# Gated results turned by VectorE and GpSimd instead of TensorE, with the first two output chunks taken in turns

## The reference

```
h = rmsnorm(x)                      # layers 2, 3: also scaled and shifted
q, k, v, ..., z = split(h @ w_in)   # 2048 -> 6400 .. 20480 columns
mixed = mixer(q, k, v, ...)         # (256, 2048)
gated = mixed * silu(z)
x = x + gated @ w_out               # layers 2, 3: times a gate row
```

## Time and profile before

| | |
|---|---|
| time, median of 3 runs (lowest, highest) | 2493.15 us (2492.67, 2493.81) |
| time of the profiled execution | 2495.73 us |
| its span, first to last instruction | 2493.9 us |
| busy: PE, DVE, ACT, POOL | 2452.6, 1703.0, 1184.6, 522.9 us |
| mean granted TensorE clock | 0.995 |
| HBM traffic over the span | 212 GB/s |

### The profile page before, as it was taken

The page is one execution under the profiler, slowest core; times in us unless marked ns, Lnnn a source line. Parts: engine busy times, 40 slices in busy tenths (PEclk is TensorE's granted clock), DMA queues, the critical chain, the costliest instruction groups (busy, mean ns, idle before and its releaser), DMA issues.

```text
span 2493.9 us, 30840 instructions
## 1 busy us (share of the span) xinstructions
PE 2452.6 (98%) x11830; PEld 2055.0 (82%) x11830; DVE 1703.0 (68%) x2086; ACT 1184.6 (48%) x1573; POOL 522.9 (21%) x692
## 2 busy tenths in 40 slices
PE   8999999999999999999999999999999989999998
PEld 7898888888888887888888888888888878888786
DVE  5887865677787776666566666666655676667665
ACT  5557654445445544344443434444454444444543
POOL 1000000134430000533153053234300023223000
PEclk9999999999999999999999999999999999999999
DMA  7545545687767875887588677768745657777654
GB/s 237 167 136 148 149 129 188 188 269 252 250 219 242 269 260 169 271 268 253 168 257 259 202 248 242 236 210 262 252 137 181 193 176 229 226 228 228 203 193 136
DMA packets 254468, 531.80 MB, mean 213 GB/s; under 512 B 16377, under 2 KB 26945, under 8 KB 254193
## 3 DMA queue, kind: packets, MB, share of 16 engines
q1 hardware_dynamic: 253120, 526.06, 66.9%
q0 software_dynamic: 896, 3.20, 0.4%
q10 hardware_dynamic: 304, 0.57, 0.1%
HBM read 527.67 MB, written 2.10 MB: 212 GB/s over the span
## 4 chain that ended last, share of the span: by engine, by line
PE 81%; issue 11%; DVE 4%; ACT 2%; POOL 1%; DMA 0%; POOLq 0%; DVEq 0%; SPq 0%; ACTq 0%
PE proj L1020 23%; PE proj L1022 23%; PE proj L1021 23%; PE att L1070 2%; PE att L1053 2%; DVE w_lo L1697 1%; PE proj L1001 1%; ACT w_hi L1298 1%; PE att L1201 1%; PE att L1117 1%; PE proj L1006 1%; POOL slot L2001 1%; PE proj L1027 1%; PE proj L1028 1%; PE proj L1029 1%
## 5 line engine op out<-in xcount | busy, mean ns | idle before, releaser
L1697 DVE TENSOR_TENSOR w_lo<-raw,w_hi 128x1024 fp32r<-128x1024 f32 x804 | 989.8, 1235 | 579.6 <-ACT w_hi L1298 575.9
L1020 PE MATMUL proj<-w_hi,h 128*128 128x512 f32 (+1 forms) x3080 | 1227.8, 399 | 5.9 <-DVE h L1844 4.5
L1298 ACT ACTIVATE w_hi<-raw 128x1024 fp32r<-128x1024 f32 x804 | 847.6, 1057 | 767.2 <-PE proj L1022 747.4
L1022 PE MATMUL proj<-w_hi,h 128*128 128x512 f32 (+1 forms) x3080 | 1199.9, 390 | 0.0
L1021 PE MATMUL proj<-w_lo,h 128*128 128x512 f32 (+1 forms) x3080 | 1197.8, 389 | 0.0
L1020 PEld LDWEIGHTS proj<-w_hi,h 128*128 128x128 f32 x3080 | 580.2, 188 | 122.2 <-issue 9.7
L1022 PEld LDWEIGHTS proj<-w_hi,h 128*128 128x128 f32 x3080 | 579.3, 188 | 123.0
L1021 PEld LDWEIGHTS proj<-w_lo,h 128*128 128x128 f32 x3080 | 580.6, 189 | 114.0 <-issue 1.7
L2001 POOL COPY slot<-stage 32x256 f32<-32x256 f32 x640 | 481.1, 752 | 816.5 <-DVE stage L1714 781.1
L1858 DVE SCALAR_TENSOR_TENSOR mod_acc<-raw,vec,mod_acc 128x1024 f32<-128x1024 f32 x192 | 255.2, 1329 | 0.3 <-DMA raw<-in_mod_w 0.3
L1987 POOL TENSOR_TENSOR row_rstd<-row_rstd,power 128x2 f32<-128x2 f32 x5 | 3.6, 716 | 569.0 <-DVE row_rstd L1788 569.0
(11 more groups left out here) (236 smaller groups left out, 1486.2 us busy)
## 6 DMA issues: line engine op xcount, KB each, us to landing
raw<-in_a_w_in SPq DMA_DIRECT2D x320, 512.0 KB, 4.7
raw<-in_mod_w SPq DMA_DIRECT2D x192, 512.0 KB, 4.4
raw<-in_w_in_odd SPq DMA_DIRECT2D x128, 512.0 KB, 4.6
raw<-in_b_w_in SPq DMA_DIRECT2D x128, 512.0 KB, 4.3
raw<-in_w_in_even SPq DMA_DIRECT2D x100, 512.0 KB, 3.7
raw<-in_w_out_even SPq DMA_DIRECT2D x32, 512.0 KB, 4.1
raw<-in_w_out_odd SPq DMA_DIRECT2D x32, 512.0 KB, 5.4
raw<-in_a_w_out SPq DMA_DIRECT2D x32, 512.0 KB, 4.0
```

What stands on the lines that cost most here:

```text
L1020: pe.matmul(o, x_hi[:, xs], hi[:, kk, :], start=start, stop=False)
L1022: done = pe.matmul(o, x_lo[:, xs], hi[:, kk, :], start=False, stop=stop)
L1298: act.activation(m.w_hi[u.n % SPLIT_N][:, 0:size], m.raw[i][:, 0:size], ACT.Copy).then_inc(s.hi_ready, 1)
L1697: dve.tensor_tensor(m.w_lo[ring][:, 0:size], m.raw[i][:, 0:size], m.w_hi[ring][:, 0:size].bitcast(F32), ALU.subtract).then_inc(s.lo_dve, 1)
```

## The change

PE's hout is gone. At each of the 16 gates DVE, after its multiplication, transposes the chunk into `stage` with two instructions (one for each tile of 128 tokens), and POOL moves it with 16 copies back into `mixed`, in place. hout keeps its ACT and DVE halves, which now read `mixed` in place of the PSUM bank and wait for `turned`; they stand five slots behind the gate, not two. The turns of gates and of q and k chunks are numbered together, and each DVE transposition waits for the turn before it. The first two output chunks are run in turns: pairs 1 to 4 of the order for chunk 0, the same for chunk 1, then pairs 5 to 8 for chunk 0 and for chunk 1. With it the residual addition of chunk 0 (`resid`) moves four slots back in every layer, and so do `masks` (layer 1) and the first `weigh` (layer 3).

```diff
+    def run_in_turns(self, chunks, early, late):
+        for pairs in (early, late):
+            for c in chunks:
+                for pair in pairs:
+                    self.units.append(Unit(len(self.units), c, pair, pair * UNIT_K, pair == early[0], pair == late[-1]))
+                c.last = len(self.units) - 1
...
+    early, late = list(order)[:PAIRS // 2], list(order)[PAIRS // 2:]
+    plan.run_in_turns(cs[:2], early, late)
+    for ch in cs[2:]:
         plan.run(ch, order)
...
-        slot = max(ready[p][0] + 2, free, before + 1)
+        slot = max(ready[p][0] + TURN_SLOTS, free, before + 1)
...
         elif kind == "hin":
             use(it, kind, it.banks, s.h_done, it.n + 1)
-        elif kind == "hout":
-            use(it, kind, it.banks, s.h_done, it.n + 1)
...
-        elif kind == "hout":
-            w.wait_ge(s.gated, it.ready)
-            for j in range(UNIT_K):
-                k = it.pair * UNIT_K + j
-                for tile in range(TILES):
-                    at = j * SEQ + tile * P
-                    done = pe.transpose(m.bank(it.banks[0], at, at + P), m.mixed[:, tile, k * P:(k + 1) * P], m.ident)
-            done.then_inc(s.h_mm, 1)
...
         elif kind == "hout":
-            w.wait_ge(s.h_mm, it.n + 1)
+            w.wait_ge(s.turned, it.chunk.turn_out)
             w.wait_ge(s.unit_done, it.h_free)
             hi = m.halves(it.n % H_RING)[0]
-            act.activation(m.in_order(hi, it.layer), m.in_tiles(m.bank(it.banks[0])), ACT.Copy).then_inc(s.h_hi, 1)
+            act.activation(m.in_order(hi, it.layer), m.mixed_pair(it.pair), ACT.Copy).then_inc(s.h_hi, 1)
...
             dve.tensor_tensor(out, out, m.token(c.slot), ALU.mult).then_inc(s.gated, 1)
+            w.wait_ge(s.gated, c.gate_n)
+            w.wait_ge(s.turned, c.turn_out - 1)
+            for tile in range(TILES):
+                blocks = m.stage[:, :].rearrange("p (g t h j) -> p t g h j", g=QUAD, t=TILES, j=FOLD)[:, tile, :, :, :]
+                done = dve.transpose(blocks, out[:, tile, :].rearrange("p (h g j) -> p g h j", g=QUAD, j=FOLD))
+            done.then_inc(s.stage_full, 1)
...
-        elif kind == "turn":
+        elif kind == "turn" or kind == "gate":
             c = it.chunk
-            w.wait_ge(s.stage_full, c.turn_n)
+            n, into = (c.turn_n, m.turn_into) if kind == "turn" else (c.turn_out, m.turn_out_into)
+            w.wait_ge(s.stage_full, n)
```

More of the change, by code:

```diff
@@ L38 @@
 AHEAD = 3
+TURN_SLOTS = 5
 HEAD_PAIRS = 2
@@ L184 @@
     turn_n: int = 0
+    turn_out: int = 0
     scaled: bool = False
@@ L228 @@
     dve_n: int = 0
+    mm_n: int = 0
     act_n: int = 0
@@ L306, in out_projection @@
     for c in range(D // CHUNK):
-        ch = plan.chunk(layer, 2 * layer + 1, w, c * CHUNK, "token", "resid", col=c * CHUNK)
+        cs.append(plan.chunk(layer, 2 * layer + 1, w, c * CHUNK, "token", "resid", col=c * CHUNK))
+    early, late = list(order)[:PAIRS // 2], list(order)[PAIRS // 2:]
+    plan.run_in_turns(cs[:2], early, late)
+    for ch in cs[2:]:
         plan.run(ch, order)
-        cs.append(ch)
     return cs
@@ L404, in halves @@
         for j in range(2):
-            ready[ch.col // 256 + j] = (gated[i], ch.gate_n)
+            ready[ch.col // 256 + j] = (gated[i], ch)
     before = 0
@@ L409, in halves @@
         free = h["last"][m - H_RING] + 1 if m >= H_RING else 0
-        slot = max(ready[p][0] + 2, free, before + 1)
+        slot = max(ready[p][0] + TURN_SLOTS, free, before + 1)
         before = slot
         assert slot < min(u.n for u in plan.units if u.chunk.phase == 2 * layer + 1 and u.pair == p), (layer, p, slot)
-        plan.at(slot, "hout", layer=layer, pair=p, n=m, banks=(2 + m % 2,), h_free=free,
-                ready=ready[p][1])
+        plan.at(slot, "hout", layer=layer, pair=p, n=m, h_free=free, chunk=ready[p][1])
         h["index"][2 * layer + 1, p] = m
@@ L572, in make_plan @@
     for c in range(D // CHUNK - 1):
-        plan.at(ends[-1] - PAIRS * (2 - c) - 4, "weigh", n=c)
+        plan.at(outs[c].last + 4, "weigh", n=c)
     plan.at(ends[-1], "final")
@@ L587, in number @@
 def number(plan, s, h):
+    turns = 0
+    for slot in sorted(plan.slots):
+        for kind, it in sorted(plan.slots[slot], key=lambda w: ORDER.index(w[0])):
+            if kind == "turn":
+                turns += 1
+                it.chunk.turn_n = turns
+            elif kind == "gate":
+                turns += 1
+                it.chunk.turn_out = turns
     out_n = {"slot": 0, "resid": 0, "feature": 0}
@@ L597, in number @@
                 c.wide_n = out_n["wide"] = out_n.get("wide", 0) + 1
-        if c.form == "turn":
-            out_n["turn"] = c.turn_n = out_n.get("turn", 0) + 1
         if c.turn_n and c.layer >= 2:
@@ L640, in number @@
         elif kind == "hin":
+            it.mm_n = n
             if it.layer >= 2:
                 it.ready = count["val"] = count.get("val", 0) + 1
-            use(it, kind, it.banks, s.h_done, it.n + 1)
-        elif kind == "hout":
             use(it, kind, it.banks, s.h_done, it.n + 1)
@@ L757, in halves, with mixed_pair, staged @@
         return self.h[:, place, :, 0, :], self.h[:, place, :, 1, :]
-    def in_tiles(self, a):
-        return a.rearrange("p (k a n) -> p k a n", k=UNIT_K, a=TILES)
+    def mixed_pair(self, pair):
+        return self.mixed[:, :, pair * UNIT_K * P:(pair + 1) * UNIT_K * P].rearrange("p a (k n) -> p k a n", k=UNIT_K)
+    def staged(self, a, g):
+        return self.stage[a * FOLD:(a + 1) * FOLD, g * TURN:(g + 1) * TURN].rearrange("p (t h j) -> p t h j", t=TILES, j=FOLD)
     def in_order(self, h, layer):
@@ L801, in turn_into, with turn_out_into @@
     def turn_into(self, c, a):
-        return self.slots[c.slot][:, :].rearrange("p (b a j) -> p b a j", a=QUAD, j=FOLD)[:, :, a, :]
+        return self.token(c.slot).rearrange("p t (h a j) -> p t h a j", h=HPC, j=FOLD)[:, :, :, a, :]
+    def turn_out_into(self, c, a):
+        return self.mixed[:, :, c.col:c.col + CHUNK].rearrange("p t (h a j) -> p t h a j", h=HPC, j=FOLD)[:, :, :, a, :]
     def keys(self):
@@ L1359, in scalar_program @@
                 if j == 1 or not it.fine:
-                    w.wait_ge(s.h_mm, it.n + 1)
+                    w.wait_ge(s.h_mm, it.mm_n)
                 ps = m.bank(it.banks[j if it.fine else 0])
@@ L1848, in vector_program @@
             hi, lo = m.halves(place)
-            dve.tensor_tensor(m.in_order(lo, it.layer), m.in_tiles(m.bank(it.banks[0])), m.in_order(hi, it.layer).bitcast(F32),
+            dve.tensor_tensor(m.in_order(lo, it.layer), m.mixed_pair(it.pair), m.in_order(hi, it.layer).bitcast(F32),
                               ALU.subtract).then_inc(s.h_done, 1)
@@ L1999, in gpsimd_program @@
                     g = (a + turn) % QUAD
-                    src = m.stage[a * FOLD:(a + 1) * FOLD, g * TURN:(g + 1) * TURN].rearrange("p (b j) -> p b j", j=FOLD)
-                    done = pool.tensor_copy(m.turn_into(c, a)[g * FOLD:(g + 1) * FOLD, :, :], src)
+                    done = pool.tensor_copy(into(c, a)[g * FOLD:(g + 1) * FOLD], m.staged(a, g))
                     if a < QUAD - 1:
@@ L2009, in gpsimd_program @@
                     w.wait_ge(s.pool_step, own.n)
-                    w.wait_ge(s.turned, c.turn_n)
+                    w.wait_ge(s.turned, n)
         elif kind == "rot_norm":
```

1 line of the change is left out of this document (removed).

## The result

| | before | after |
|---|---|---|
| time, median (lowest, highest) | 2493.48 us (2492.67, 2494.34), 4 runs | 2480.88 us (2479.68, 2481.91), 4 runs |
| profiled execution, its span | 2495.73, 2493.9 us | 2479.68, 2477.9 us |

The change makes the kernel faster by 12.6 us; the ratio is 0.9949 [0.9937, 0.9961].

A forecast was written before the change was run, and what follows sets the result against it. PE's issue time was taken to bound the output projections. Gains of 14.7, 1.4, 0.8 and 1.7 us (18.6) less 4.2 lost in layer 0 gave -14.4: 2481.3 us profiled, 2478.8 as a median, range 2475 to 2486.

The forecast's parts named there:

- Issue time, -14.7: Output projections: PE no longer issues 32 houts' transposes, 27 at 0.48 us and five at 0.35, gaining 14.7 us.
- Bank waits, -1.4 and -0.8: PE's waits for a hout's lo half at L1119 and L1090 vanish, gaining 1.4 of 1.9 us and 0.8 us.
- DVE's two transpositions, 1.36 us: At each of 16 gates DVE's two added transpositions take 1.36 us together; no loss to PE was counted.
- Case (c): Rival: DVE's 1.36 us at eight gates among attention steps each cost PE in full; 2489.7 us, no change; chance 0.08.
- Copies into `mixed`: POOL's 16 copies a gate take the same durations as its existing copies, 0.445 us each where DVE is idle.
- rival (b): Copies into `mixed` take longer, turns slower by a factor; gain gone at 1.36, 2505 us at 1.6; chance 0.08.
- Layer 0: Last two gates: the second waits for an 8.6 us turn, so PE waits 2.5 us at unit 105; 4.2 lost with clock.
- Rival (a): Layer 0's turn takes 13.45 us, PE waits 7.4 and the loss is 9.1 us; 2483.7 us; chance 0.20.
- The clock, -1.7 and +1.7: PE's low clock behind L1119's wait goes, gaining 1.7 us; one behind layer 0's new wait comes, losing 1.7.
- case (d): Layer 0's clock doesn't fall or unit 105's split slips in earlier; 2476 to 2477 us; shares chance 0.62 with main forecast.
- Layers 1 to 3, "cost: nothing": Last gate of each layer: a turn may take 16.2 us before PE waits, even 15.50 fits, so nothing is lost.
- The offset of 2.6 us between the profiled execution and the median: The profiled execution before was 2.6 us over the median; subtracting this turned 2481.3 into 2478.8 us.

The follow-up runs named there:

- no_transpose: The kernel before with nobody transposing the gated results, order and spacing unchanged, so the output projection multiplies a wrong matrix; 2472.66 us, ratio 0.9919 to before.
- Experiment 5: The changed kernel with the old order of output chunks and houts two slots behind the gate, not five; 2507.82 us, ratio 1.0062 to before.
- Experiment 3: The changed kernel with layer 0's last gate transposing into another free buffer, so it does not wait for the first turn; 2478.0 us, ratio 0.9944 to before.
- order_only: The kernel before with only the new order in turns of the first two output chunks, transposes kept on PE; 2493.15 us, ratio 1.0 to before.
- experiment 4: The changed kernel with houts six slots behind their gate, not five; 2480.29 us, ratio 0.995 to before.
- experiment 7: The changed kernel with houts six slots behind the gate and layer 0's last gate keeping its eight transposes on PE; 2475.1 us, ratio 0.9925 to before.

## Why the prediction was right, and where it was off

2478.8 us was forecast, in a range of 2475 to 2486, and 2480.88 measured; in differences, -14.4 and -12.6.

2480.88 us lies inside the range, but not every term held: two terms for the clock were wrong and cancelled, and a loss that was put at nothing was in part made up by gains that were larger than forecast. That the difference came within 2 us is to that extent luck.

**Issue time, -14.7: right.** Units start 2.72 us apart, and each hout between two weight matmuls gives back 0.48 to 0.49 us. no_transpose, with nothing put in the transposes' place, bounds all gains together: 18.9 us in the ledger, of which the issue time and the two bank waits of the sum are 16.9.

**Bank waits, -1.4 and -0.8: right.** For L1119's wait of 1.9 us a rest of 0.5 was foreseen, for DVE's copy that now stands behind the gate's transpositions. The rest is what L1144 waits for that same copy (L1681 now): 0.28 us by the printed wait, 0.5 by the ledger (a step of -2.04 us, and -2.58 in no_transpose).

**DVE's two transpositions, 1.36 us: right.** They take 1.30. Case (c) did not come: at the early gates, where the forecast took nothing, attention steps lose this 0.5 us in layer 0 and 0.4 at L1248 in layer 3 (the wait is 0.8 in no_transpose and 1.2 in every kernel that turns that gate), not 10.9.

**Copies into `mixed`: right.** The 256 of them take 180.8 us, 706 ns each, against 752 ns for those into a slot, and those that fall in DVE's idle time take 390 to 400 ns. So the factor of rival (b) is not above 1, and its mechanism is absent. The turns took 8.99 to 15.25 us, two of them above the 14 that stood among the signs. The Trainium skill's rule (VectorE: DVE Perf Modes, Rules for kernel authors) to give a 128x128 transposition to TensorE did not hold here: TensorE's issue bounds the time (98% busy), and the two engines that took it over were busy for only 70% and 28% of it. Experiment 5 shows that turns can nevertheless make this kernel slower: for want of distance, not of speed.

**Layer 0: right in mechanism, 0.7 us short in size.** A wait of 2.5 us was forecast, 3.20 measured. The turn took 8.99 us and not 8.6. And it began 8.37 us before PE came to the unit (370.54, and 382.11 - 3.20 = 378.91), not 8.65. Together 0.7. The second part comes from the gate: it starts 0.15 us behind the first weight matmul of unit 101 (367.92 and 367.77), where before it started 0.37 ahead of it (374.60 and 374.97). Of these 0.5 us, 0.2 are given back, as the printed wait takes PE to come that much later than the pitch of 2.72 has it. Why the gate came later was not tried. Rival (a) with its turn of 13.45 us did not come, for the reason that stood against it: DVE is blocked in just this stretch. Experiment 3 is the counter-test: with DVE not blocked, the turn took 12.71. (That most turns of before take 13.45 us is not so either: of the 40, 22 took less, from 8.98 to 13.39, and nine 13.45 or 13.46.)

**The clock, -1.7 and +1.7: both wrong as steady terms.** The low clock behind the 1.9-us wait was a property of that execution: a second one of the same kernel and order_only have the same wait of 1.88 us, and 1.00 behind it. Behind the wait of 3.20 us in after the clock stayed up, behind 3.79 and 7.26 us in experiments 4 and 5 it fell. In the sum the two terms cancelled, so the forecast did not suffer by it; that is luck. In layer 0 it went as case (d) has it, and yet the time did not go below 2477, since (d) too had counted the gained clock and left out the next point.

**Layers 1 to 3, "cost: nothing": the step that was off, by 1.9 us in layer 1.** The bound itself held. It said that the turn may take 16.2 us from a start 5.2 us after unit 260 (861.3 and 856.1), that is, end 21.4 after it. Measured: start 9.7 (856.42 less 846.70), length 13.38, end 23.1, 1.7 too late; PE had by then slipped by 0.5 already, and waited 0.86. What was wrong was the start, taken from the gate of before. The working looked at what the *last* turn lets ACT do late, and not at the third gate's, whose hout stands ahead of the evacuation from which the last gate starts. That a turn makes the gate late is borne out by experiment 2, where nothing is turned and the gate starts 2.5 us after unit 260; that PE's 1.36 us are lost because this turn ends too late for the houts, by experiment 4, where the gate is almost as late, the houts have a unit more, and 0.4 us of the loss is left. A kernel with five slots and the gate in time, which would show the late gate to be the whole cause, was not run. The other 0.5 us, behind the wait of 0.20 at unit 261, went with it; which of the two, ACT's shorter stall or the later hout, did that was not tried apart. The step of the working that failed is thus the start of the last turn, 5.2 us after unit 260, where 9.7 was measured. In layers 2 and 3 no wait came; their third turns took 12.76 us.

**The offset of 2.6 us between the profiled execution and the median.** It was carried over as a constant. The second execution of before is 3.5 us shorter than the first: 1.3 us of it is the start (the first weight matmul at 66.04 us in the one execution of before, 64.79 in the other), and 1.6 the clock (against the first execution the ledger's step at the weight matmuls of 353.89 is -2.04, against the second -0.46), and the rest stands near 952 us.

What was measured, against the profiled execution of before: spans 16.0 apart, less 1.66 for the start (64.38 for 66.04) and 1.6 for the low clock: -12.8, where -16.9 + 2.5 = -14.4 was forecast. The missing 1.6 us is layer 1's 1.9 and layer 0's 0.7, less some 1 us that the gains were better.

Among the chances, faster by more than 5 us should have had 0.62 + 0.20 + 0.02 = 0.84 and not 0.86, as case (c) was put at no change.

## What to carry to other kernels

Where TensorE is the limit, small transposes are worth what the pitch of the work around them loses (0.48 us for four), not their duration (0.27 us each), and idle engines can take them even if they need ten times as long and more (a chunk of eight: 0.96 us on TensorE, 8.99 to 15.25 us a turn); but only with distance between the one who makes and the one who uses. Here 2 slots cost 13.9 us, 5 slots gained 12.6, and a reordering of the consumer that is worth nothing by itself is what makes room for the distance. Where two such jobs come one slot apart and share an engine, a second buffer moves the wait (2.1 us for 3.2) and does not remove it: leave one of them where it was (experiment 7). And when a wait is put on an engine that walks a fixed list, follow each item behind it, also that from which the *next* such job starts.

## What the runs showed of the hardware

A low clock behind an idle time of TensorE is not certain at a given length: after 1.9 us idle the next stretch had 0.58 in one execution and 1.00 in two others, after 3.20 us 1.00, after 3.79 us 0.74, after 7.26 us 0.50. A term of the sum that rests on one such stretch should be carried as a chance.

A POOL copy of 32x256 took 390 ns at the least and 1497 at the most; of the first four of layer 0's turn at 370.54 three began in DVE's idle time and took 390 to 396 ns, and the one beside DVE's split took 1282. DVE's operations slow less: the split there took 1.29 us and the gate 1.41, where both took 1.22 to 1.23 before. So the length of a turn, 8.99 to 15.25 us for the same 16 copies, goes with what DVE does in that time; experiment 3, where the same turn takes 12.71 us once DVE is not blocked, shows it. The Trainium skill (GPSIMD Engine Reference, Key points) says that GpSimd shares its SBUF interfaces with VectorE and contends with VectorE's instructions that have two SBUF inputs. The split and the gate are of that kind, and the trace agrees: 1282 ns beside the split, 390 to 396 without.

The start of the program, ahead of the first weight matmul, ended at 62.35 us in order_only's profiled execution, at 64.79 and 66.04 in those of before. From there on order_only and the second of before run alike to 0.2 us over the whole span (2488.1 and 2490.4). In the stretch from 24 to 28 us the granted clock was 1.00 in order_only, 0.75 in the second of before and 0.61 in the first, in the order of their starts. So part of the 5 us by which single runs of before differ (2489.55 to 2494.56) may arise ahead of all that the change touches.
